# A two-part transformer kernel: GpSimd taken out of the stage meetings, column groups for thin products, other shares of rows, and four reorderings

## Time and profile before

| | us |
|---|---|
| median of 3 runs | 3609.58 (3601.81 to 3609.76) |
| the profiled execution's own time | 3620.59 |
| its span, first to last instruction | 3618.8 |
| PE busy | 2789.4 (77% of the span) |
| DVE busy | 2228.3 (62%) |
| POOL busy | 1162.5 (32%) |
| ACT busy | 581.0 (16%) |
| mean rate of all transfers | 284 GB/s |

### The profile page before, as it was taken

One profiled execution on the slowest core, in us unless ns is written; L12 is line 12 of the kernel. 1 busy time (PEld: TensorE's weight loads), 2 busy tenths in 40 slices (PEclk: granted clock), 3 DMA queues, 4 the chain that ended last, 5 costly groups with the idle time before them and its releaser, 6 DMA issues. The chain is left out here.

```text
span 3618.8 us, 31432 instructions
## 1 busy us (share of the span) xinstructions
PE 2789.4 (77%) x10098; PEld 1781.8 (49%) x10098; DVE 2228.3 (62%) x5250; ACT 581.0 (16%) x1595; POOL 1162.5 (32%) x1028
## 2 busy tenths in 40 slices
PE   8894768689957867998688587777779857787776
PEld 1573646478846466887457232322236733332222
DVE  0339676655556757555677687665546377766555
ACT  0221120210002102000131111111113211111111
POOL 0000344234443532344231344444410014444442
PEclk9997877789979968999799799999989979899999
DMA  8422677569978755899454799999952239999997
GB/s 321 150 72 95 229 269 243 178 212 354 348 259 311 272 171 191 325 342 357 150 176 144 319 418 420 421 420 421 421 213 70 72 153 420 421 421 421 421 418 309
DMA packets 208228, 1026.34 MB, mean 284 GB/s; under 512 B 23240, under 2 KB 24488, under 8 KB 141760
## 3 DMA queue, kind: packets, MB, share of 16 engines
q0 software_dynamic: 147456, 805.37, 57.0%
q1 hardware_dynamic: 59744, 214.69, 16.4%
q10 hardware_dynamic: 864, 4.28, 0.3%
HBM read 1020.53 MB, written 3.72 MB: 283 GB/s over the span
## 5 line engine op out<-in xcount | busy, mean ns | idle before, releaser
L2146 PE MATMUL ps<-w_ring,diag 128*128 128x512 f32 x1216 | 578.8, 623 | 171.4 <-ACT diag L2109 171.1
L1255 POOL DMA_INDIRECT ctx_ring<-in_peer_u,ctx_expert x256 | 305.5, 1193 | 891.6 <-POOLq L162 514.0
L2029 DVE SCALAR_TENSOR_TENSOR w_ring<-w_ring,htok 128x1024 f32<-128x1024 f32 x304 | 371.9, 1224 | 237.8 <-DMA w_ring<-in_peer_uv,expert 237.3
L2146 PEld LDWEIGHTS ps<-w_ring,diag 128*128 128x128 f32 x1216 | 228.3, 196 | 517.7 <-ACT diag L2109 276.7
L2146 PE MATMUL ps<-own,diag 128*128 128x512 f32 x624 | 313.5, 644 | 205.2 <-ACT diag L2109 205.2
L2016 POOL DMA_INDIRECT w_ring<-in_peer_uv,expert x304 | 333.1, 1096 | 408.2 <-PE ps L2146 396.7
L1267 DVE SCALAR_TENSOR_TENSOR ctx_ring<-ctx_ring,h_now 128x1024 f32<-128x1024 f32 x256 | 306.6, 1224 | 125.3 <-DMA ctx_ring<-in_peer_u,ctx_expert 116.8
L2016 POOL DMA_INDIRECT own<-in_peer_uv,expert x156 | 166.6, 1068 | 637.8 <-POOLq L162 367.8
L1255 POOL DMA_INDIRECT ctx_ring<-in_peer_v,ctx_expert x208 | 249.0, 1197 | 284.8 <-DVE sum L1271 120.6
L1173 PE MATMUL ps<-mix,w_ring 128*128 128x256 f32 x1408 | 313.1, 384 | 14.0 <-DVE mix L360 8.2
L2146 PEld LDWEIGHTS ps<-own,diag 128*128 128x128 f32 x624 | 118.1, 201 | 394.5 <-ACT diag L2109 278.5
(11 more groups left out here) (395 smaller groups left out, 4110.7 us busy)
## 6 DMA issues: line engine op xcount, KB each, us to landing
w_ring<-in_weights SPq DMA_DIRECT2D x392, 512.0 KB
w_ring<-in_peer_uv,expert POOLq DMA_INDIRECT x304, 15.8
ctx_ring<-in_peer_u,ctx_expert POOLq DMA_INDIRECT x256
ctx_ring<-in_peer_v,ctx_expert POOLq DMA_INDIRECT x208
own<-in_peer_uv,expert POOLq DMA_INDIRECT x156, 15.8
consts_sb<-in_consts ACTq DMA_DIRECT2D x1, 1867.0 KB, 9.9
cT_first<-in_ctx_by_feature ACTq DMA_DIRECT2D x1, 1024.0 KB
xT<-in_x_by_feature ACTq DMA_DIRECT2D x1, 1024.0 KB
```

Source lines behind the costliest of these rows:

```text
L1255: pool.indirect_dma_start(out=m.ctx_ring[:, r % CTX_RING, :], out_offset=None, in_=expert_tables(self.d)[r // SLOTS], in_offset=bass.Indir ...
L2029: v.scalar_tensor_tensor(out=u, in0=u, scalar=1.0, in1=m.htok[:, blk, :], op0=ALU.mult, op1=ALU.mult, accum_out=b.dots[:, e:e + 1]).then_i ...
L2146: ins = pe.matmul(m.ps[:, 2 * blk + half, :], b.diag[:, e % DIAGS, :], entry(e)[:, D + half * 512:D + (half + 1) * 512], start=(k == 0), s ...
```

## The change

1. **One block.** `stage` no longer opens a block. All stages share one `nc.Block()`, and at the end of a stage PE, ACT, DVE and SP meet on one semaphore, `joined`. The names take their semaphores from two halves used in turn, and SP clears a half with one instruction after the meeting. POOL is not in the meetings: it gets the list of all 512 context rows once, and in `peer_experts` it waits for the meeting by itself.
2. **Weights.** PE's wait and increment after each group are gone; SP waits for the stage's own product semaphore.
3. **Column groups.** The products with two columns become `column_group_products`: two steps of four products, each into its own 32 PSUM partitions (the stationary operand padded with zeros to 32 columns). The four partial sums are added later by a matmul with a pick matrix. In `rwkv` one step stands before a level's update and one after it. The copies out of PSUM have 128 partitions; four small transfers replace one.
4. **Rows.** `ContextRows` and `ContextTail` become one list with one ring; the shares change; the weights move from `feed_forward` to the start of `out_projection`; `feed_forward` takes 4 rows per tile instead of 3.
5. **Order on ACT and DVE.** A Sqrt on one column stands ahead of `norm_act` and of `out_projection`'s squares; in `rwkv` the Sigmoids stand ahead of the Tanh; the mask of the next level stands ahead of the wait for the update (`select_level`).
6. **Memory.** `peer_experts` has one own entry and two in the context ring; the context's `qT` lies in that ring.

```diff
@@ stage
-        with nc.Block() as block:
-            yield block, s, b
-        for n in names.split():
-            nc.sync.sem_clear(s[n])
-        nc.all_engine_barrier()
+        yield m.block, s, b
+        m.stages += 1
+        def join(eng):
+            eng.drain().then_inc(m.joined, 1)
+            eng.wait_ge(m.joined, JOINING * m.stages)
...
+        @m.block.sync
+        def _(sp):
+            join(sp)
+            sp.sem_clear(range(first, first + len(names)))
@@ WeightRing.load_to
-            if g >= WSLOTS:
-                eng.wait_ge(self.mem.w_used, g - WSLOTS + 1)
+            if done and g - WSLOTS >= g0:
+                eng.wait_ge(*done(g - WSLOTS - g0))
@@ norm_act
+    act.activation(b.rstd[:, 0:1], m.const("eps"), ACT.Sqrt)
@@ in_projection (the same in the other stages with weights)
-                if j + 1 == len(tiles) or tiles[j + 1][0] != g:
-                    pe.wait_ge(s.prod_done, j + 1)
-                    pe.sem_inc(m.w_used, 1)
@@ rwkv
-            act.activation(b.th[:, 0, :], m.pf[:, 6, :], ACT.Tanh).then_inc(s.acted, 1)
             for j in range(2):
                 act.activation(b.sg[:, j, :], m.pf[:, 7 + j, :], ACT.Sigmoid).then_inc(s.acted, 1)
+            act.activation(b.th[:, 0, :], m.pf[:, 6, :], ACT.Tanh).then_inc(s.acted, 1)
...
-                mod_part(lev, 0, 2)
+                mod_part(lev, 0, 1)
...
+            for lev in range(1, LEVELS):
+                rows.take(v, 6, "rwkv")
+                if lev + 1 < LEVELS:
+                    v.wait_ge(s.w_done, lev + 1)
+                    select_level(lev + 1)
                 v.wait_ge(s.upd_done, lev)
@@ out_projection
+            if weigh_rows:
+                gelu_tanh(act, s, b.th[:, :], 1)
+            act.activation(m.root[:, 0:1], m.const("eps"), ACT.Sqrt)
@@ ContextRows
-    SHARE = dict(in_projection=26, rwkv=70, latent_heads=4, attention=14, out_projection=12, feed_forward=106)
+    SHARE = dict(in_projection=32, rwkv=72, latent_heads=8, attention=16, out_projection=12, feed_forward=92)
+    TAIL_SHARE = dict(project_qkv=12, attention=14, out_projection=12, peer_queries=10)
...
+        pool.wait_ge(m.joined, JOINING * m.stages)
+        for r, (blk, v, k) in enumerate(self.order):
+            if r >= CTX_RING:
+                pool.wait_ge(m.ctx_used, r - CTX_RING + 1)
@@ new
+def column_group_products(pe, m, bank, w, k0, k1):
+    for k in range(k0, k1):
+        for q in range(COLUMN_GROUPS):
+            ins = pe.matmul(m.ps[GROUP * q:GROUP * (q + 1), bank, :], m.silu[:, 2 * q + k, :], w[:, 2 * q + k, :],
+                            start=(k == 0), stop=(k == 1), skip_group_check=True)
+    return ins
@@ modulation
-                        ins = pe.transpose(m.ps[:, 2, c:c + 2], b.row[:, (g - 1) % 2, j * P:(j + 1) * P], m.ident[0:2, 0:2])
+                        ins = pe.matmul(m.ps[:, 2, c:c + 2], b.row[:, (g - 1) % 2, j * P:(j + 1) * P], b.pick[:, :],
+                                        start=True, stop=True)
```

More of the change, by code:

```diff
@@ L675, in _ @@
             link(v.memset(b.state[:, 0, :, :], 0.0))
-            rows.take(v, 4)
+            rows.take(v, 4, "rwkv")
             v.wait_ge(s.acted, 5)
@@ L691, in _ @@
             v.sem_inc(s.ready_bonus, 1)
-            rows.take(v, 3)
+            rows.take(v, 3, "rwkv")
             v.wait_ge(s.kk_root, 1)
@@ L739, in _ @@
                 t, q = c // 2, c % 2
-                rows.take(v, 4 if c else 2)
+                rows.take(v, 4 if c else 2, "rwkv")
                 v.wait_ge(s.sa_done, c + 1)
@@ L760, in _ @@
                          s.y_copied)
-            rows.take(v, 2)
+            rows.take(v, 2, "rwkv")
             v.wait_ge(s.mean_done, 1)
@@ L920, in _ @@
         def _(sp):
-            ring.load_to(sp, g0 + G_OUT + WSLOTS)
-        @block.gpsimd
-        def _(pool):
-            rows.fetch(pool, "latent_heads")
+            ring.load_to(sp, g0 + G_OUT + WSLOTS, g0 + G_UQ, lambda n: (s.prod_done, (3, 7)[n]))
         @block.tensor
@@ L1015, in _ @@
             wide = lambda i: m.ps[:, i, :].rearrange("p (f t) -> p f t", f=2)
-            rows.take(v, 3)
+            rows.take(v, 3, "latent_heads")
             v.wait_ge(s.rope_done, 3)
@@ L1121, in _ @@
                 if rows:
-                    rows.take(v, 2)
+                    rows.take(v, 2, "out_projection")
             if rows:
@@ new lines, in __init__ @@
+    def __init__(self, m, d):
+        self.m, self.d = m, d
+        kept = SLOTS - CTX_TAIL
+        self.order = [(blk, v, k) for blk in range(TT) for v, n in ((0, SLOTS), (1, kept)) for k in range(n)]
+        self.order += [(blk, 1, k) for blk in range(TT) for k in range(kept, SLOTS)]
+        self.taken = 0
+        self.ends, at = {}, 0
+        for l, share in enumerate((self.SHARE, self.SHARE, self.TAIL_SHARE)):
+            for name, n in share.items():
+                at += n
+                self.ends[l, name] = at
+        assert at == len(self.order) == TT * 2 * SLOTS
@@ L1329, in expert_tables, with weigh @@
+        self.take(v, self.ends[self.l, name] - self.taken, name)
+    def weigh(self, v, link, s, th):
+        m, l = self.m, self.l
+        assert self.order[self.taken][1] and self.order[self.taken][2] == 0
+        v.wait_ge(m.ctx_used, self.taken)
+        gelu_weights(v, link, s, th, m.ctx_dots[:, :], m.ctx_weight[:, l, :], m.ctx_weight[:, l, :], 1)
+        link(v.memset(m.tail_sum[l], 0.0))
 def expert_tables(d):
@@ L1405, in write_out @@
 def write_out(nc, m, d):
-    with stage(nc, "written") as (block, s, b):
+    with stage(m, "written") as (block, s, b):
         @block.sync
```

385 lines of the change are left out of this document (156 added, 229 removed).

## The result

The changed kernel takes 3556.8 us (median of 4 runs, 3555.5 to 3559.8) against 3609.7 us: a ratio of 0.9857, 95% interval 0.9841 to 0.9874. It is faster by 53 us, where 147 were forecast (3463 us), and lies outside the range of 3425 to 3521. A second set of five runs gave the same ratio, 0.9857 (0.9834 to 0.9880). The profiled execution has a span of 3558.0 us against 3618.8: 60.8 us less. That is the number that the stages must add up to.

The account below looks back on a forecast made before the run. Each stage had its own limit: transfers in `peer_experts`, PE in `feed_forward`, a chain in `rwkv`. Terms -30 - 28 - 83 - 17 + 23.4 - 12 = -146.6 us gave 3474 on the profiled execution, 3463 on the median; range 3425 to 3521.

Parts of the forecast that it names:

- Meetings, -30: All stage ends: one meeting on one semaphore instead of two barriers and clears per name, -30 us, bounds -24 and -38.
- Column groups in `modulation`, -28: Modulation's thin products: four column groups stream side by side, so transfers set the pace instead of PE, -28 us.
- The drain: TensorE draining at a change of tiling mode, about 4 times per group in `rwkv`: 0.68 us each, 33 us, not summed.
- `feed_forward`, -83: Both layers: stops at weight groups and the tail of rows behind PE go, rows ending 4 us late: -83 us.
- rival C: `feed_forward`: rows become the bound, transfers stay at 0.88, the tail shrinks by half only: 3491 us; chance 0.14.
- The stops: PE's waits for its own product at group changes, 0.68 us each: -11.6 us in layer 0's `feed_forward`, -9 elsewhere.
- `rwkv`, -17: Both layers: scan starts 5 us earlier, levels 6 us shorter, end 2.4 us longer: -8.6 us per layer.
- Rival B: `rwkv` levels: PE cools to half clock in pauses, +47 us against -17, half of it likely: 3493 us; chance 0.12.
- Rows elsewhere, +23.4: Both layers, more rows taken: `in_projection` +6.5 per layer, `latent_heads` +4, `first_attention` +1.2; +23.4 us in all.
- The Sqrt ahead of the norms, +1: Norm starts: early table load gains nothing, Sqrt delays first square 0.2 us six times, +1; load behind meeting: bound +8.
- rival D: `peer_experts`: gathers lose rate, each 1% costing 13 us; at 13% 3635 us, slower than before; chance 0.03.
- The good ends: Whole kernel: all favourable bounds of the terms together, put at -185 us, the fast end of the range.

## Why the prediction was wrong, step by step

- **Meetings, -30.** Right: 0.25 us behind `rwkv`, where 2.71 stood before, and 31 us less between stages in all. No experiment was made on it.
- **Column groups in `modulation`, -28.** Right in size and in cause: -29.1 with the meeting at its end (-29 forecast), and +30 when undone. The drain that the prediction priced at 0.68 us, and left out of the sum, costs some 0.1 us and was there before (last section).
- **`feed_forward`, -83: the step that failed; it gave -27 with the meetings, where -87 was forecast.** "PE's part is 230 us" was nearly right (233 with 3 rows, 236 for the stage without the last 26 rows). Two readings failed. The first, that 4 rows per tile would leave PE alone: I read the tail and the bytes and never laid 4 rows against one tile. A row costs the ring 2.5 us, four cost 10 us against PE's 7, and the release of PE's bank stands behind them. That was 11 us a layer, and no rival named it. The second was "the rows end 4 us late": 83 MB at 369 GB/s. With 3 rows per tile the stage moved 85 MB in 255 us, a mean of 333 GB/s: its first 20 us ran at a share of 0.47 with both rings full, and the rest at 0.89 to 0.97. That was rival C, at 20 us a layer where its text said 14.
- **The stops, -11.6 a layer inside it and -9 elsewhere.** Too dear: 0.5 us, not 0.68, so 8.6 us a layer of PE's part, which the rows behind PE take back. Elsewhere no run shows them alone.
- **`rwkv`, -17 without the meetings; it gave -5.** The start gave 4 us (scan 7.5 us after the first instruction, against 11.4), of which 2 were left at the end of the first level. The next four levels gave 4.2 (by the experiments 2.5 to 3.7 from the column groups and 1.8 from the masks), forecast 6 with the first level. The first chunk came 2.8 and 2.2 us later, beside a lower clock, and the stretch behind the last chunk grew by 2.2 and 0.6 us without the meeting (2.4 forecast for its rows). Rival B was right about the mechanism, and too dear.
- **Rows elsewhere, +23.4; they gave about +34.** `in_projection` +17, forecast 13, and within its scatter. `latent_heads` gave +19, forecast 8: a row was taken for 1.15 us a row of VectorE's time; four landed ones cost that, the eighth waited 5.9 us behind weights.
- **The Sqrt ahead of the norms, +1, and the load ahead of the meeting.** This reading failed: the load waits for the meeting, each of five norms starts 1.4 us later, and the Sqrt costs 6 to 7 us. That is the case at which the bound of +8 was put.
- **The experts' gathers (rival D)** kept their 0.98. The first of them took 664 us, more than 5 over the 657 named as a sign of being wrong, but it had taken 663 before.
- **The numbers of the range.** The good ends as stated add up to -209, not -185, and half of rival B's 47 is 24, not 30. Neither brings 3556.8 inside.

## What to carry to other kernels

A tail of background work moved among an engine's products costs nothing only where the engine that does it was waiting; compare, per step of the loop, what the background costs in its slowest resource (here 2.5 us for a row to land) with the step itself, and look what is queued behind it on that engine. When a stage is bound by bytes, moving them inside it changes little, and a stage with room for transfers is not enough: 24 rows moved to such stages gave nothing, since they ended those stages, while 10 rows a layer moved to where VectorE waited for PE were free. Where rings stand full, free their slots early. Price a stop by the length of the phase with it and without it, not by the idle time of one engine. And look what a reordered instruction itself waits behind.

## What the runs showed of the hardware

- Four products of 32 columns on different column groups overlap: 16 take 1.92 to 3.64 us, one alone 0.59 to 1.06 us, and 16 full ones 7.3 us.
- By the Trainium skill, "TensorEngine Tiling (Array Packing)", Key Properties, a change between 32- and 128-column work drains TensorE. The trace agrees, and the cost is small. Full products that follow each other start 0.14 to 0.21 us ahead of the modelled end of the last one, also from one line of the kernel to another; at each change the next one starts only 0.07 us ahead of it (L567's 16 end at 495.22, and the next starts at 495.15). So a change costs some 0.07 to 0.14 us, an estimate from modelled ends. The two-column products of the kernel before show the same 0.07 us, so the column groups add no such changes. Full products in turn (0.17 us of overlap), and at their end a change (0.07):

```profile
496.33 0.49 PE L578 MATMUL ps<-ws,invT 128*128 128x128 f32 x2
496.65 0.39 PE L579 MATMUL ps<-invT,ws 128*128 128x128 f32 x2
...
499.78 0.39 PE L579 MATMUL ps<-invT,ws 128*128 128x128 f32 x2
500.10 1.06 PE L1439 MATMUL ps<-w_ring,silu 128*32 128x512 f32 x8
```

- A wait of PE for its own last product costs 0.30 us, and 0.47 us with a semaphore increment behind it (down products), while the load behind it shows 0.68 us of idleness and the product 0.31.
- An ACT_TABLE_LOAD (1.28 us) begins ahead of the wait of its own function for its input (113.92), but not ahead of the meeting (342.55 above).
- With 4 rows of 0.52 MB in flight beside weights, a row lands every 2.5 us, also when VectorE does nothing else.
